# Second attention: the decays as a table in every query's partition, added where the mask was added

## The reference

```python
ck = jnp.moveaxis(cb, 2, 1)[..., None, :]          # cumulative log-forget values, per key and head
s = jnp.einsum('bqhd,bkhd->bhqk', qblk, kb).astype(jnp.float32) * SCALE
decay = jnp.moveaxis(cqblk, 2, 1)[..., :, None] - ck
visible = kpos[None, :] <= qp[:, None]
pm = jax.nn.softmax(jnp.where(visible, s + decay, NEG_INF), axis=-1)
return jnp.einsum('bhqk,bkhd->bqhd', pm.astype(vb.dtype), vb)
```

## Time and profile before

| | us |
|---|---|
| three runs, median | 1268.1 (1268.03 to 1268.12) |
| profiled execution | 1268.2, its span 1266.2 |
| DVE busy | 748.7 (59%) |
| ACT busy | 561.1 (44%) |
| POOL busy | 187.4 (15%) |
| second attention | from about 963.5 to 1005 us of the span |

### The profile page before, as it was taken

How to read it: one execution, slowest core, us unless ns; L and a number is a source line. 1 busy time by engine, 2 the same in 40 slices (tenths; PEclk the granted TensorE clock), 3 DMA queues, 4 the chain that set the end, 5 groups by cost and what they waited for, 6 DMA issues and landing times.

```text
span 1266.2 us, 22363 instructions
## 1 busy us (share of the span) xinstructions
PE 1256.4 (99%) x8756; PEld 1238.8 (98%) x8756; DVE 748.7 (59%) x1127; ACT 561.1 (44%) x829; POOL 187.4 (15%) x206
## 2 busy tenths in 40 slices
PE   9999999999999999999999999999999999999999
PEld 9999999999998999999999999999997899999999
DVE  7766575554777656564544775654456765556433
ACT  6543453344376543433353444333355754343322
POOL 0120021146143000000132000001134420000000
PEclk9999999999999999999999999999999999999999
DMA  8364445646214444454454534355440134444343
GB/s 307 136 180 136 166 144 162 209 168 196 102 35 162 139 162 137 161 179 142 139 176 144 198 134 165 133 166 164 157 166 34 69 133 167 138 160 136 134 141 129
DMA packets 41069, 190.17 MB, mean 150 GB/s; under 512 B 4592, under 2 KB 15248, under 8 KB 25904
## 3 DMA queue, kind: packets, MB, share of 16 engines
q1 hardware_dynamic: 37296, 183.43, 42.3%
q0 software_dynamic: 1184, 3.13, 1.2%
q10 hardware_dynamic: 2528, 2.77, 0.9%
HBM read 182.38 MB, written 6.94 MB: 150 GB/s over the span
## 4 chain that ended last, share of the span: by engine, by line
PE 98%; ACT 1%; DVE 1%; DMA 0%; issue 0%; SPq 0%; DVEq 0%; ACTq 0%
PE bank L523 30%; PE bank L525 30%; PE bank L524 30%; PE bank L937 1%; PE bank L760 1%; PE bank L799 1%; PE bank L802 1%; PE bank L769 1%; PE outs L549 0%; PE outs L836 0%; PE outs L551 0%; DMA x<-in_xT 0%; PE bank L571 0%; ACT ew L1349 0%; PE outs L533 0%
## 5 line engine op out<-in xcount | busy, mean ns | idle before, releaser
L523 PE MATMUL bank<-xhi,whi 128*128 128x320 f32 (+1 forms) x1760 | 545.6, 310 | 1.1 <-DVE wlo L1999 0.9
L525 PE MATMUL bank<-xhi,wlo 128*128 128x320 f32 (+1 forms) x1760 | 543.0, 309 | 0.0
L524 PE MATMUL bank<-xlo,whi 128*128 128x320 f32 (+1 forms) x1760 | 543.0, 309 | 0.0
L1609 DVE TENSOR_TENSOR wlo<-raw,whi 128x2048 fp32r<-128x2048 f32 (+1 forms) x176 | 361.6, 2054 | 236.8 <-ACT whi L1168 236.6
L1168 ACT ACTIVATE whi<-raw 128x2048 fp32r<-128x2048 f32 (+1 forms) x177 | 304.4, 1720 | 327.6 <-PE bank L525 321.9
L523 PEld LDWEIGHTS bank<-xhi,whi 128*128 128x128 f32 x1760 | 330.5, 188 | 3.6 <-issue 1.9
L524 PEld LDWEIGHTS bank<-xlo,whi 128*128 128x128 f32 x1760 | 330.6, 188 | 0.5
L525 PEld LDWEIGHTS bank<-xhi,wlo 128*128 128x128 f32 x1760 | 330.5, 188 | 0.0
L523 PE MATMUL bank<-hhi,whi 128*128 128x320 f32 x704 | 217.7, 309 | 0.0
L525 PE MATMUL bank<-hhi,wlo 128*128 128x320 f32 x704 | 217.5, 309 | 0.0
L524 PE MATMUL bank<-hlo,whi 128*128 128x320 f32 x704 | 217.5, 309 | 0.0
(11 more groups left out here) (237 smaller groups left out, 1040.1 us busy)
## 6 DMA issues: line engine op xcount, KB each, us to landing
raw<-in_w_ffn_in SPq DMA_DIRECT2D x85, 1024.0 KB, 4.8
raw<-in_w_ffn_out SPq DMA_DIRECT2D x64, 704.0 KB, 4.1
raw<-in_w_in_a SPq DMA_DIRECT2D x10, 1024.0 KB, 4.8
raw<-in_w_out SPq DMA_DIRECT2D x8, 1024.0 KB, 4.8
raw<-in_w_kv SPq DMA_DIRECT2D x6, 1024.0 KB, 4.8
raw<-in_w_mkv SPq DMA_DIRECT2D x4, 1024.0 KB, 4.7
raw<-in_w_in_b SPq DMA_DIRECT2D x4, 1024.0 KB, 4.8
raw<-in_w_ffn_in SPq DMA_DIRECT2D x6, 256.0 KB, 6.3
```

Of the source, the lines that this page charges most:

```text
L523: mm(acc, wh, mhi(ks[q]), start=start and q == 0, stop=False)
L524: mm(acc, wh, mlo(ks[q]), start=False, stop=False)
L525: last = mm(acc, wl, mhi(ks[q]), start=False, stop=stop and q == nk - 1)
L1609: tt(wlo[slot][:, 0:size], raw[slot][:, 0:size], f32(whi[slot][:, 0:size]), ALU.subtract).then_inc(lo_ready[slot], 1)
```

## The change

Before the attention the decays are written to DRAM as 12 rows of 832 values, and two loads on ScalarE's queue repeat them over the partitions: `decays_b` holds, for each query partition, the decays of its head in all six units (6 x 832). It lies where the first attention's query blocks lay. GpSimd adds the triangle of the causal mask to the last 64 columns of each chunk, for all six units at once, five additions, and these stand in its program between the square for `pb_q` tile 4 and the attention. VectorE's maxima of the fox units read `decays_b` instead of `causal`; before the first of them it waits for the five additions. The two decay matmuls of each fox unit are gone, with them the low part of `dec` and the zeros, and the fox scores start their banks themselves.

```diff
-                        if first and i >= 2 and not fox:
+                        if first and i >= 2:
                             pe.wait_ge(s_taken, 2 * (u - 2) + b + 1)
-                        if fox and n == 0:
-
-                            pe.wait_ge(s_taken, 2 * (u - 2) + 2)
-                            for bank, lo, w in ((0, 0, 384), (1, 384, 448)):
-                                mm(pair[bank][:, 0:w], pair_of(unit["tile"]), dec[:, lo:lo + w], start=True, stop=False)
...
-            def decays_hi(j):
-
-                if j != 2:
-                    return
-                act.wait_ge(zeroed, 2)
-                for q, (lo, w) in enumerate(((0, 384), (384, 448))):
-                    f = AUX0["dec"] + q
-                    act.wait_ge(aux_ready, f + 1)
-                    nc.scalar.activation(dec[0:H_B, lo:lo + w], aux[f % 2][0:H_B, 0:w], ACT.Copy
-                                         ).then_inc(dec_hi, 1)
+            def decays_out(j):
+
+                if j == 2:
+                    for q, (lo, w) in enumerate(((0, 384), (384, 448))):
+                        f = AUX0["dec"] + q
+                        act.wait_ge(aux_ready, f + 1)
+                        nc.scalar.activation(dec[0:H_B, lo:lo + w], aux[f % 2][0:H_B, 0:w], ACT.Copy
+                                             ).then_inc(aux_free, 1)
+                    act.wait_ge(aux_free, AUX0["dec"] + 2)
+                    act.dma_start(dec_out[:], dec[0:H_B, :]).then_inc(d_dec_out, 16)
+                if j == 3:
+                    act.wait_ge(d_dec_out, 16)
+                    for e in range(2):
+                        act.dma_start(decays_b[HD * e:HD * e + HD],
+                                      bass.AP(dec_out.tensor, e * DEC, [[0, HD], [2 * DEC, 6], [1, DEC]])
+                                      ).then_inc(d_dec, 16)
...
                         elif unit["kind"] == "fox":
-                            add = causal[:, low:low + keys]
+                            if i == 3 and bank == 0:
+                                dve.wait_ge(dec_masked, 5)
+                            add = decays_b[:, unit["tile"], 384 * b + at:384 * b + at + keys]
...
-            def decays_lo(j):
-                if j != 3:
-                    return
-                for q, (lo, w) in enumerate(((0, 384), (384, 448))):
-                    f = AUX0["dec"] + q
-                    dve.wait_ge(dec_hi, q + 1)
-                    tt(dec[32:32 + H_B, lo:lo + w], aux[f % 2][0:H_B, 0:w], f32(dec[0:H_B, lo:lo + w]), ALU.subtract
-                       ).then_inc(aux_free, 1)
...
-            pool.wait_ge(acc_ready, TILE0["pb"])
-            nc.gpsimd.memset(dec[:].bitcast(F32), 0.0).then_inc(zeroed, 1)
             head_squares_lo("pb_m", lambda j: qk[:, 6 + j, :], R, acc_free, lambda j: TILE0["pb"] + j + 1)
             head_squares_lo("pb_q", lambda j: qk[:, j, :], R, acc_free, lambda j: TILE0["pb"] + 2 + j + 1, range(5))
+            pool.wait_ge(d_dec, 32)
+            for _, b, at, _, keys in CHUNKED:
+                own = decays_b[:, :, 384 * b + at + keys - 64:384 * b + at + keys]
+                nc.gpsimd.tensor_tensor(own, own, causal[:, 192:256].unsqueeze(1).broadcast_to([P, 6, 64]), ALU.add
+                                        ).then_inc(dec_masked, 1)
             attention(1)()
```

More of the change, by code:

```diff
@@ L204, in encoder_kernel @@
             sb("under", [P, 4 * 640], F32, region)
+        with ExitStack() as region:
+            decays_b = sb("decays_b", [P, 6, DEC], F32, region)
         qz = sb("qz", [P, 8, 5, P])
@@ L271, in encoder_kernel @@
         rows_out = nc.dram_tensor("rows_out", [4, 12, R], F32, kind="Internal").ap()
+        dec_out = nc.dram_tensor("dec_out", [H_B, DEC], F32, kind="Internal").ap()
         scratch = nc.dram_tensor("bias_scratch", [64, H_A, NREL + 1], F32, kind="Internal").ap()
@@ L359, in encoder_kernel @@
         d_turns = sem("d_turns")
-        dec_hi = sem("dec_hi")
+        d_dec_out = sem("d_dec_out")
+        d_dec = sem("d_dec")
+        dec_masked = sem("dec_masked")
         lf_step = sem("lf_step")
@@ L759, in scores @@
                                 for k, to in keyed:
-                                    last = mm(pair[b][own, at + to:at + to + k.shape[-1]], q, k, start=not fox,
-                                              stop=not fox or last_of[b] == n and to == keyed[-1][1])
+                                    last = mm(pair[b][own, at + to:at + to + k.shape[-1]], q, k, start=True, stop=True)
                         elif unit["kind"] == "mem":
@@ L1573, in _ @@
             ffn_out("out2", "attn_1", "pb")
[L1574 to L1583 removed]
+            def decays_out(j):
[13 more added lines that the diff above has]
+                                      ).then_inc(d_dec, 16)
             projection("pb", R, [("pb_m", 0), ("pb_q", 2)], 8, tile_b, {3: "pb_m"}, True,
[L1586 removed]
+                       after=decays_out, before=lambda j: exps_b() if j == 7 else None)
             attention_b()
```

4 lines of the change are left out of this document (1 added, 3 removed).

## The result

The changed kernel takes 1280.3 us (median; 1279.0 to 1280.7) where the kernel before takes 1268.2 on the same chip: a ratio of 1.0093, 95% interval 1.0082 to 1.0104. The profiled execution took 1280.2 us with a span of 1278.2, against 1266.2 before. The forecast was 1275.8 with a range of 1270.2 to 1279.5: the sign and the place were right, the size was 4.5 us short, and the measured time lies 0.8 us above the range.

The account below looks back on a forecast made before the run. TensorE, busy 99% of the span, was taken as the bound. From 1268.1 us: + 6.4 stall + 1.6 slower clock - 0.3 gain = 1275.8, range 1270.2 to 1279.5.

Parts of the forecast that it names:

- I take 964.5: Broadcasts of the decay table on ScalarE's queue: both landed at 964.5, between ends of 958.0 and 967.
- The mechanism: Unit 0 of the attention: GpSimd's wait, additions and scaling delay TensorE's third transpose and everything behind it by 6.4 us.
- The additions: GpSimd behind its wait for the landing: five adds of 0.95 us each, 4.75 us.
- The clock: TensorE behind the idle: the clock falls to the lower level, costing 1.6 us.
- the first leg: Scores of unit 1 after the restart: at the slow clock they take twice 1.94 us, what follows ends 1.6 later.
- The gain: Forgetting units: of 2.8 us of removed TensorE products 0.3 us arrives, as ScalarE's rows leave no gap.
- VectorE's maxima read the table where they read the mask: no cost: VectorE's maxima in the forgetting units: same count and same length with the table, so no cost.
- C: Rival: table lands later, 967 to 970, with all engines reading it and a weight load; 1278.3 to 1281.5 us; chance 0.12.
- A: Rival: TensorE's clock stays at 2.4 GHz after the idle; 1274.2 us; chance 0.20.
- D: Rival: TensorE's clock stays low up to the first query row, +4.9 us; 1279.1 us; chance 0.09.
- B: Rival: broadcasts run at the weight loads' rate, stall 2.5 us, no clock fall; 1270.3 us; chance 0.13.
- F: Rival: GpSimd's wait lands where nobody stands behind it, time as before; chance 0.03.

Follow-up runs that it names:

- the busy run: Changed kernel with 62 matmuls of 320 columns into an unused score bank between unit 0's second and third transpose: 1279.1 us, ratio 1.0081.
- after: The profiled execution of the changed kernel, against the kernel before: 1280.2 us with a span of 1278.2.

## Why the prediction was wrong, and what of it was right

- **The step that failed is the time of the landing**, the term "I take 964.5". The second half landed at 968.0, and 3.5 of the 4.5 us that were missing are this. The working had 967 as its other end, with 2 us for a weight load in the same stretch, and then left that load out of the value it took, although the load stood in the stretch from 954 to 955 of the earlier trace rows. Held back, the load gave 3.0 us, and the second half landed at 965.0.
- **That 965.0 is so near to 964.5 is in part luck.** The working took 246 GB/s in mid-transfer as the keys' broadcasts showed it, and the table by itself moved at 207 to 215. On the other side it multiplied by 2.6 a time of 5.0 us that also held the stretch between the last data and the landing; for the table, with 2.6 times the bytes, that stretch was only some 2 us (share 0.08 from 966 to 968). The two errors go against one another, and no run parts their sizes.
- **The mechanism was right in each link**: GpSimd waits for the landing, five additions, the scaling behind them, TensorE's third transpose behind that, then the clock's fall, and everything after it shifted. The sum of the measured terms is 10.0 + 2.1 - 0.1 = 12.0 us, the difference of the spans. The sum of the forecast was 6.4 + 1.6 - 0.3 = 7.7.
- **The additions** were sized well: 4.79 us for the five, where 4.75 were forecast. The stall was 3.6 us longer than forecast, 3.5 by the landing and 0.1 by the small gaps around the additions.
- **The clock** cost 2.1 us and not 1.6; the busy run settles it. I had priced the first leg alone (the scores of unit 1). TensorE's starts show the rest: against the kernel before, the two transposes took 0.4 us more, the scores 1.7, the head statistics 0.5, and the wait before the query row shrank by 0.5 (1.31 to 0.77).
- **The gain** was 0.1 us and not 0.3. The reading that ScalarE's rows without idle let nothing through was right, but not the whole of it: with them relieved only 0.35 us came.
- **"VectorE's maxima read the table where they read the mask: no cost"** was right; the run with the additions later and left out shows that table, store, broadcasts and reads, with the products gone, cost 0.0 to 0.3 us.
- **The rivals**: C (a later landing through the weight load, 1278.3 to 1281.5) was the one that came, with 0.12, and most of its interval lay outside the range I gave; the clock staying up (A) and a slow clock up to the query row at 4.9 us (D) are refuted by the rows, and so is a landing at the weight loads' rate (B). In the chances, F and half of B make 0.095 and not 0.08.
- **What no rival had**: moving the additions off the path does not make them free. In the run with the additions moved they cost 3.5 us of span (4.1 less the early shift of 0.6), the clock's fall included; put in alone, 1.6 us (1.8 less a shift of 0.2) where the clock stayed up, and 4.5 to 4.9 in the executions with the lower mean clock.

## What to carry to other kernels

A wait put into an engine's program costs what stands behind it there, so count the landing with every transfer that runs in the same stretch, and the idle's echo in TensorE's clock (about 2 us here). Before a small job is moved to a "free" GpSimd, read what VectorE does in that stretch: 4.1 us of additions held up its scalings of SBUF tiles by 2.0 us, and beside instructions with one operand in PSUM nothing was seen. And work taken off the busiest engine inside a tight round of four engines is worth only the gap to the next one: 2.8 us of matmuls were worth 0.1.

## What the runs showed of the hardware

- GpSimd's additions (128 x 384, two inputs in SBUF, 0.99 us) against VectorE: a pair of 128 x 256 scalings in SBUF takes 1.36 to 1.90 us instead of 0.62, a 64 x 320 step with both inputs in SBUF 1.16 to 1.27 instead of 0.48, one with a PSUM input 0.48 as ever. The additions themselves take up to 1.25 then.
- The granted clock fell after idles of 9.9, 5.9, 4.7 and 3.6 us, and also after two idles of 1.35 and 2.26 us with 0.66 us of work between them; behind a single idle of 3.5 us (974.35, above) it was 0.50 as well. With idles of 1.00 and 1.18 us (the additions alone) it stayed at 1.00 in the profiled execution; three other executions of that kernel have a mean clock of 0.997. The fall cost 2.1, 1.8 and 1.4 us behind idles of 9.9, 5.9 and 3.6.
- A table written to 64 partitions at a time moved at 207 to 215 GB/s; to 128 partitions, all reading the same rows, at 334 to 346, and at 407 together with a load; in blocks of 16 by 8 from copies of the rows at 226 together with a load and at 238 to 265 alone; at a DMA share of 0.12, at 53.
- The semaphore of a half came some 2 us after its last data: the DMA share was 0.08 from 966 to 968 in after (landing 968.0), and 0.06 from 963 to 965 with the load held back (landing 965.0).
